# Down weights of a mixture-of-experts kernel loaded as column halves instead of row halves

## The reference

```python
def hier_moe(h, w_group, b_group, w_router, b_router, w_gate, w_up, w_down):
    ...
    out = jnp.zeros_like(ht)
    for e in range(N_EXPERTS):                       # 32 experts
        hid = jax.nn.silu(ht @ w_gate[e]) * (ht @ w_up[e])    # 2048 -> 512
        out = out + gates[:, e:e + 1] * (hid @ w_down[e])     # 512 -> 2048
    return out.reshape(b, s, d)
...
x = x + g2 * hier_moe(...)
return rmsnorm(x, final_g)
```

## Time and profile before

| | us |
|---|---|
| median of 3 runs | 1585.63 (1585.49 to 1586.74) |
| the profiled execution, its time | 1588.13 |
| its span, first to last instruction | 1586.3 |
| TensorE busy | 1368.7 (86% of the span) |
| VectorE busy | 551.7 |
| ScalarE busy | 141.0 |
| GpSimd busy | 53.0 |
| mean granted TensorE clock | 0.953 |

### The profile page before, as it was taken

The page is one execution under the profiler, slowest core; times in us unless marked ns, Lnnn a source line. Parts: engine busy times, 40 slices in busy tenths (PEclk is TensorE's granted clock), DMA queues, the critical chain, the costliest instruction groups (busy, mean ns, idle before and its releaser), DMA issues.

```text
span 1586.3 us, 14991 instructions
## 1 busy us (share of the span) xinstructions
PE 1368.7 (86%) x6048; PEld 702.7 (44%) x6048; DVE 551.7 (35%) x864; ACT 141.0 (9%) x394; POOL 53.0 (3%) x62
## 2 busy tenths in 40 slices
PE   4569999997789967988988988988988988988985
PEld 3138888875578854332332332332332322332331
DVE  2015365417654443215214224224224224223225
ACT  2010000007610011000000000000000000000001
POOL 1000000000000000000000000000000000000000
PEclk9789999999999988999999999999999999999998
DMA  9999999994278820899999999999999999999992
GB/s 346 393 394 389 392 365 388 364 366 168 86 240 304 304 101 27 338 424 428 425 425 430 424 425 428 425 426 430 423 426 428 426 425 430 424 425 429 425 424 101
DMA packets 108543, 572.61 MB, mean 361 GB/s; under 512 B 5785, under 2 KB 61225, under 8 KB 62553
## 3 DMA queue, kind: packets, MB, share of 16 engines
q1 hardware_dynamic: 106504, 568.15, 89.1%
q0 software_dynamic: 2000, 3.95, 0.9%
HBM read 569.89 MB, written 2.18 MB: 361 GB/s over the span
## 4 chain that ended last, share of the span: by engine, by line
PE 63%; DMA 27%; DVE 5%; issue 2%; ACT 2%; SPq 1%; DVEq 0%; POOL 0%; POOLq 0%; ACTq 0%
PE PS L1189 21%; DMA ring<-in_w_up 16%; PE PS L1210 11%; PE PS L1169 8%; PE PS L1116 7%; PE PS L1043 7%; DMA ring<-in_w_ada 5%; DMA ring<-in_w_qkv 5%; PE PS L1151 2%; PE PS L1052 2%; PE PS L994 2%; DVE W L929 1%; DVE W L717 1%; PE PS L1087 1%; DMA r<-in_x 1%
## 5 line engine op out<-in xcount | busy, mean ns | idle before, releaser
L1189 PE MATMUL PS<-ring,W 128*64 128x512 f32 x1024 | 240.7, 628 | 39.2 <-DMA ring<-in_w_up 39.1
L1210 PE MATMUL PS<-ring,W 128*64 128x512 f32 x1024 | 233.6, 610 | 26.8 <-DVE W L929 17.7
L1189 PE MATMUL PS<-ring,gysq 128*64 128x512 f32 x1024 | 225.9, 597 | 14.3 <-DMA ring<-in_w_up 10.8
L1043 PE MATMUL PS<-r,ring 128*128 128x256 f32 x800 | 176.9, 384 | 2.5 <-DMA ring<-in_w_qkv 2.5
L1189 PEld LDWEIGHTS PS<-ring,W 128*64 128x64 f32 x1024 | 81.4, 145 | 192.7 <-issue 192.7
L1043 PEld LDWEIGHTS PS<-r,ring 128*128 128x128 f32 x800 | 153.7, 193 | 26.1 <-DMA ring<-in_w_qkv 3.2
L717 DVE SCALAR_TENSOR_TENSOR W<-ring,sm,W 128x2048 f32<-128x2048 f32 x60 | 141.0, 2351 | 65.1 <-DMA ring<-in_w_ada 63.6
L907 DVE TENSOR_TENSOR r<-r,PS 128x512 f32<-128x512 f32 x128 | 88.0, 687 | 203.0 <-PE PS L1169 203.0
L1210 PEld LDWEIGHTS PS<-ring,W 128*64 128x64 f32 x1024 | 75.8, 140 | 163.5 <-issue 138.2
L1189 PEld LDWEIGHTS PS<-ring,gysq 128*64 128x64 f32 x1024 | 76.4, 138 | 161.6 <-issue 161.6
L1169 PE MATMUL PS<-W 128*128 128x512 f32 x256 | 128.5, 641 | 21.3 <-DVE W L929 21.3
(11 more groups left out here) (203 smaller groups left out, 668.9 us busy)
## 6 DMA issues: line engine op xcount, KB each, us to landing
ring<-in_w_gate SPq DMA_DIRECT2D x64, 2048.0 KB, 25.0
ring<-in_w_up SPq DMA_DIRECT2D x64, 2048.0 KB, 26.9
ring<-in_w_down SPq DMA_DIRECT2D x64, 2048.0 KB, 26.1
ring<-in_w_ada SPq DMA_DIRECT2D x48, 2048.0 KB, 25.0
ring<-in_w_qkv SPq DMA_DIRECT2D x17, 2048.0 KB, 21.0
ring<-in_w_o SPq DMA_DIRECT2D x8, 2048.0 KB, 8.2
ring<-u_scr SPq DMA_DIRECT2D x2, 2048.0 KB, 17.9
r<-in_x SPq DMA_DIRECT2D x1, 2048.0 KB, 12.3
```

The lines of the kernel that those rows point to most:

```text
L1043: last = mm(ps[:, sub * T:(sub + 1) * T], w[:, t, sub * P:(sub + 1) * P], hT[:, t, :], start=(t == 0), stop=(t == KT - 1))
L1189: last = mm(PS[64 * j:64 * j + 64, i % 2, :].rearrange("p (m n) -> p m n", m=2), hE[i % 2][:, k], w[:, :, t, 256 * j:256 * j + 256], start ...
L1210: last = mm(PS[64 * q:64 * q + 64, 4 + i2, :], hidT[:, b, 64 * j:64 * j + 64], w[:, b, 512 * ch:512 * ch + 512], start=(j + b == 0), stop= ...
```

## The change

The down weights of an expert come as the left and the right 1024 output columns, each with all 512 rows: chunk 4 + c is for each partition four runs of 4 KB, at a distance of one row of 128 x 8 KB. A chunk now completes one PSUM bank, so `result` works in four operations of 64 x 512, two after each chunk, and the waits of `down` are by bank. `BACK` gives the new order of scatter, adds and squares: the left half of the columns for both token halves, then the right half. The waits of the last norm follow that order.

```diff
--- before.py
+++ after.py
@@ -69,6 +69,8 @@
 DN_AT = [GROUP.index((i, 4)) for i in range(4)]
 GU_END = [k + 4 for k in GU_AT]
 DN_END = [k + 2 for k in DN_AT]
+
+BACK = [(h, 2 * c + q) for c in range(2) for h in range(H) for q in range(2)]
 
 
 C_ID, C_TRI, C_ONE = 0, P, 2 * P
@@ -382,7 +384,8 @@
                     v = (gate_v, up_v)[k % 2]
                     t0 = (k // 2) * (KT // 2)
                     return (slot(s).rearrange("p (t n) -> p t n", n=FE), v[e, :, t0:t0 + KT // 2, :])
-                return (slot(s).rearrange("p (t n) -> p t n", n=D), down_v[e, :, 2 * (k - 4):2 * (k - 4) + 2, :])
+                n0 = (k - 4) * (D // 2)
+                return (slot(s).rearrange("p (t n) -> p t n", n=D // 2), down_v[e, :, :, n0:n0 + D // 2])
 
             for m in range(EXP_CHUNKS * E):
                 if m < RING:
@@ -639,14 +642,14 @@
                         expert_group(E // 4 * r + g)
                 act.wait_ge(acc_ok, 4 * E * ROUNDS + 1)
 
-            for h in range(H):
-                for ch in range(4):
-                    act.wait_ge(acc_ok, 8 * (E // 2 - 1) + 4 * h + ch + 2)
-                    A.activation(sqr, acc[:, h, 512 * ch:512 * ch + 512], ACT.Square,
-                                 accum_out=part[:, h, ch:ch + 1]).then_inc(f_ms, 1)
-                    act.wait_ge(f_ms, 4 * h + ch + 1)
-                act.wait_ge(f_rt, h + 1)
-                A.activation(rstd[:, h:h + 1], rstd[:, h:h + 1], ACT.Sqrt).then_inc(f_r, 1)
+            for k, (h, ch) in enumerate(BACK):
+                act.wait_ge(acc_ok, 8 * (E // 2 - 1) + k + 2)
+                A.activation(sqr, acc[:, h, 512 * ch:512 * ch + 512], ACT.Square,
+                             accum_out=part[:, h, ch:ch + 1]).then_inc(f_ms, 1)
+                act.wait_ge(f_ms, k + 1)
+                if ch == 3:
+                    act.wait_ge(f_rt, h + 1)
+                    A.activation(rstd[:, h:h + 1], rstd[:, h:h + 1], ACT.Sqrt).then_inc(f_r, 1)
 
 
         @block.vector
@@ -900,8 +903,7 @@
                                     EQ[:, h].rearrange("p (e s) -> p e s", e=4), gt4, ALU.mult).then_inc(sel_ok, 1)
 
             def acc_add(p):
-                for k in range(2 * 4):
-                    h, ch = k // 4, k % 4
+                for k, (h, ch) in enumerate(BACK):
                     dve.wait_ge(sc_ps, 8 * p + k + 1)
                     a = acc[:, h, 512 * ch:512 * ch + 512]
                     V.tensor_tensor(a, a, PS[:, 6 + k % 2, :], ALU.add).then_inc(acc_ok, 1)
@@ -921,13 +923,14 @@
 
             def result(g, i):
 
-                dve.wait_ge(pe_chunk, PE0 + 24 * g + DN_END[i])
                 ydv = yd.rearrange("p (i q n) -> p i q n", i=2, q=2)
                 g2v = g2b.rearrange("p (i q n) -> p i q n", i=2, q=2)
-                for q in range(2):
-                    rows = slice(64 * q, 64 * q + 64)
-                    V.tensor_tensor(ydv[64 * (i % 2):64 * (i % 2) + 64, :, q, :], PS[rows, 4:6, :],
-                                    g2v[rows, :, q, :], ALU.mult).then_inc(yd_ok, 1)
+                for c in range(2):
+                    dve.wait_ge(pe_chunk, PE0 + 24 * g + DN_AT[i] + c + 1)
+                    for q in range(2):
+                        rows = slice(64 * q, 64 * q + 64)
+                        V.tensor_tensor(ydv[64 * (i % 2):64 * (i % 2) + 64, c, q, :], PS[rows, 4 + c, :],
+                                        g2v[rows, c, q, :], ALU.mult).then_inc(yd_ok, 1)
 
             build_sel(0, 0)
             for t in range(1, KT, 2):
@@ -966,7 +969,7 @@
 
             dve.wait_ge(fg_in, 16)
             for h in range(H):
-                dve.wait_ge(f_ms, 4 * h + 4)
+                dve.wait_ge(f_ms, BACK.index((h, 3)) + 1)
                 link(V.reduce_sum(ssum[:, h:h + 1], part[:, h, 0:4], axis=AX.X))
                 V.tensor_scalar(rstd[:, h:h + 1], ssum[:, h:h + 1], 1.0 / D, EPS, ALU.mult, ALU.add).then_inc(f_rt, 1)
                 dve.wait_ge(f_r, h + 1)
@@ -1161,9 +1164,9 @@
 
             def scatter(p):
                 pe.wait_ge(selT_ok, p + 1)
-                pe.wait_ge(yd_ok, 4 * p + 4)
-                for k in range(8):
-                    h, ch = k // 4, k % 4
+                for k, (h, ch) in enumerate(BACK):
+                    if k % 4 == 0:
+                        pe.wait_ge(yd_ok, 8 * p + 6 + k // 2)
 
                     pe.wait_ge(acc_ok, 8 * p + max(1, k))
                     mm(PS[:, 6 + k % 2, :], selT[:, h * P:(h + 1) * P], yd[:, 512 * ch:512 * ch + 512],
@@ -1199,16 +1202,14 @@
 
                 def down(i):
                     pe.wait_ge(hidT_ok, 4 * g + i + 1)
-                    if i % 2:
-                        pe.wait_ge(yd_ok, 8 * g + 2 * i)
-                    for j in range(2):
-                        w = slot(chunk_at(g, DN_AT[i] + j)).rearrange("p (b n) -> p b n", b=2)
-                        for b in range(2):
-                            for i2 in range(2):
-                                for q in range(2):
-                                    ch = 2 * i2 + q
-                                    last = mm(PS[64 * q:64 * q + 64, 4 + i2, :], hidT[:, b, 64 * j:64 * j + 64],
-                                              w[:, b, 512 * ch:512 * ch + 512], start=(j + b == 0), stop=(j + b == 2))
+                    for c in range(2):
+                        if i % 2:
+                            pe.wait_ge(yd_ok, 16 * g + 4 * i - 2 + 2 * c)
+                        w = slot(chunk_at(g, DN_AT[i] + c)).rearrange("p (b n) -> p b n", b=4)
+                        for b in range(4):
+                            for q in range(2):
+                                last = mm(PS[64 * q:64 * q + 64, 4 + c, :], hidT[:, b % 2, 64 * (b // 2):64 * (b // 2) + 64],
+                                          w[:, b, 512 * q:512 * q + 512], start=(b == 0), stop=(b == 3))
                         last.then_inc(pe_chunk, 1)
 
                 gate_up(0)
```

## The result

| | us | against before |
|---|---|---|
| before, 7 runs | 1586.03 (1585.49 to 1588.07) | |
| after, 7 runs | 1591.97 (1590.63 to 1594.16) | ratio 1.0035, 95% interval 1.0025 to 1.0045 |
| after again, beside later experiments, 7 runs | 1592.27 | ratio 1.0031, 1.0020 to 1.0043 |

The change makes the kernel slower, by 5 to 6 us. The profiled execution has a span of 1590.1 us.

The account below looks back on a forecast made before the run. The prediction took the expert stage to be bound by the DMA engines' throughput. From 1585.6 us, +9.0 for packets and -4.3 at the end gave 1590.3 us, +0.30%, range 1584.5 to 1595.0.

Parts of the forecast that it names:

- The bound: Expert stage: bound by the DMA engines' throughput, share 1.01 at 426 GB/s; at the end TensorE and VectorE alone.
- Term 1: Down weight loads: 4 KB packets cost each engine 9.4 ns more apiece, 0.15 us a chunk, 9.0 us over 60 chunks.
- bounds of 5.6 and 12.7 us: Limits of Term 1, from the extreme rates of 16 and 8 KB runs: 5.9 and 13.1 ns a packet.
- Term 2: End, after the last weights: the finer order shortens three waits, together 4.3 us saved.
- (a): Last down(3): waits only for the transposed hidden, starting about 1553.95 instead of 1555.69, 1.75 us saved.
- (b): Last scatter: starts as down(3) ends; the last add ends 8.7 us after it instead of 11.1, 2.35 us saved.
- (c): Last norm: two squares instead of four behind the first root, but VectorE's scalings limit the gain to 0.2 us.
- Rival 1: Down loads: 4 KB packets cost no more by the byte than 8 KB; 1581.3 us, faster; chance 0.09.
- rival 2: Down loads: a packet costs three 32-byte beats, 3.6 ns, so 3.4 us, net -0.9: 1584.7 us; chance 0.10.
- Rival 3: End: the finer order's gain is not had, leaving 9.0 us alone, 1594.6 us; chance 0.08.
- Rival 4: Down loads: half rows read slower from memory, 391 instead of 421.6 GB/s, 1613 us; chance 0.09.
- Rival 5: TensorE's clock: about 5 us more idling a group could cost the end a microsecond or two; no separate chance.

Follow-up runs that it names:

- experiment 5: Kernel before with its last group written out; only there down(2) and down(3) by columns, finer waits and new end order: 1582.61 us against 1587.15, ratio 0.9973.
- experiment 1: Kernel before with only the column-half loads and bank-by-bank down; results, scatter, adds and norm unchanged: 1598.09 us against 1587.15, ratio 1.0077.
- experiment 3: Kernel before with two neighbouring down rows to a partition, written in eight reversed pieces of 2 KB: 1615.11 us against 1587.46, ratio 1.0187.
- experiment 2: Kernel before with two neighbouring whole down rows to a partition, written in four reversed pieces of 4 KB: 1598.10 us, ratio 1.0074.

## Why the prediction was right

It forecast 1590.3 us, +0.30%; measured were 1591.97 us, +0.35%, and +0.31% in the second measurement.

- **The bound.** Right: the DMA share stayed at 1.01 and the time followed the engines' rate. Most of what TensorE saved in the groups became waiting for weights (50.0 to 80.1 us), and experiment 5, which drops the saving in seven groups of eight, loses nothing by it.
- **Term 1, forecast 9.0 us.** The stage grew by 8.8 us in both traces of the changed kernel, by 9.0 with the column halves alone. The last two `gate_up(3)` start 119.2 us apart (1409.89 and 1529.13), against 118.1 before (1403.12 and 1521.19): 1.2 us a group, as forecast. The price of 9.4 ns a packet, taken from stretches of 16, 8 and 1 KB runs, met the rates of the 4 KB runs (409 forecast, 408 to 410 measured) and nearly those of 2 KB (383, measured 386). The bounds of 5.6 and 12.7 us (its own figures give 12.6 for the second) were wider than needed. The 6.1 ns from the output weights was the misleading figure.
- **Term 2, forecast 4.3 us.** E - G fell by 4.1 us. (a) `down(3)` starts 8.1 us after `down(2)` instead of 9.7, so 1.5 us against 1.75: it waited 0.66 us for the hidden and started 0.25 us after the copy's end, where 0.05 were reckoned. (b) The last add ends 8.7 us after `down(3)`, as worked out. (c) The second reduction starts at 1583.55, as VectorE ends its scalings: 0.2 us.
- **Rival 1 and rival 2** (packets free, or at 3.6 ns) fell by experiments 1 and 3. The runs show 9 to 10 ns a packet in saturated loads. The Trainium skill (DMA: Bandwidth & Descriptors, section Why small descriptors are slow) gives about 3 bus cycles a packet, by the prediction's estimate 3.6 ns; the runs show more than two and a half times as much.
- **Rival 3** (no gain at the end) fell by experiment 5. **Rival 4** (half rows read slower) fell by experiment 2, at 410 GB/s for both ways.
- **Rival 5**, the clock: no harm at the end of the changed kernel. In the window 1553 to 1571 its granted clock is 1.00. In the groups the clock did fall: behind the wait of 4.82 us the first half of the last `gate_up(3)` took 8.76 us instead of 7.09, as it does in most groups of the kernel before; it then waited another 1.04 us for its weights, so nothing was lost. Where the prediction has TensorE idle about 5 us more a group, its wait for weights grew by about 4.
- **What the prediction missed** is the other side of the clock. Where the waits of 2.1 to 2.7 us for VectorE are kept, the clock can fall behind them. In the seven traces with these waits, 23 of 54 `down(3)` took 8.6 to 8.8 us instead of 7.09, and 26 of the 54 scatters behind them took 9.1 to 10.6 instead of 7.70. Behind the short waits of the finer order (at most 0.75 us), all 18 `down(3)` took 7.09. The end of the kernel before, from which term 2 was read, was one at full clock; three of the five traces that keep the waits in the last group lose 1.5 to 1.7 us there. So the finer order may be worth more on average than the 4.1 us read. By these shares it would be 1.5 us more, an estimate: 23/54 of 1.7 and 26/54 of 1.6. The runs' times do not settle it: experiment 5 gives 4.3 us (2.7 to 5.9), and the changed kernel against experiment 1 gives 7 us, with some 3 of uncertainty. If it is so, the total should have been 8.8 - 5.6 = 3.2 us, where 4.9 and 5.6 were measured, so something else would have to add 2 us; that the total met the forecast would then be in part luck.

## What to carry to other kernels

Where the DMA engines are full, count packets: an edit that halves the run length of a transfer has a price even at 8 KB. One that doubles it, by giving neighbouring rows to one partition, is a small gain (0.16% here) at no cost where the order of the rows is free. In a stage that the DMA engines bound, a finer order of compute is worth something only behind the last transfer that is waited for; put it there alone, and leave the long runs everywhere else. The price of a run length that a kernel doesn't use yet can be read from two that it does; look first whether they lie on one line, as they did here. And a trace holds many copies of the same work: before a wait is priced from its last one, look at the others, since some may have met a lower clock.

## What the runs showed of the hardware

- HBM to SBUF loads with full queues on one core: 428 GB/s in runs of 16 KB, 422 in 8 KB, 409 in 4 KB, 386 in 2 KB and 347 to 371 in 1 KB. All but the 371 GB/s of the output weights fit one line, 9 to 10 ns a packet on each of 16 engines.
- A destination written in descending pieces and a source of which every other 4 KB is skipped run at the same rate (410 GB/s both).
- TensorE's granted clock can fall to its lower level (1.2 GHz) after waits of only 2.1 to 2.7 us in a stretch that is otherwise busy. It was 0.50 in the first 2.1 us after such a wait, with 32 records in 8.60 us instead of 7.09, and 23 of 54 copies of this work met it. It can also be low as a stage starts (0.70 in the mean of 10 us, 16.62 instead of 13.95 us), in two of nine traces.
